# Gate and up weights of an expert in one array: 16384-byte runs in one transfer for the first 48 experts

## What is computed

```python
hb = jax.nn.silu(xb @ we_gate[e]) * (xb @ we_up[e])
return (hb @ we_down[e]).astype(jnp.float32) * wrow[:, None]
```

## Time and profile before

| | |
|---|---|
| three runs | 1462.86, 1464.38 (median), 1465.65 us |
| profiled execution | 1464.3 us, its span 1462.5 us |
| TensorE busy | 1390.4 us (95%) |
| VectorE, ScalarE, POOL busy | 794.4, 372.3, 619.7 us |
| TensorE clock granted, mean | 0.987 |
| DMA | 322.22 MB in 123758 packets; q1 257.80 MB, q0 63.65 MB |
| chain that ended last | DMA 31%, of which the scatters 29%; TensorE 27% |

### The profile page before, as it was taken

How to read it: one execution, slowest core, us unless ns; L and a number is a source line. 1 busy time by engine, 2 the same in 40 slices (tenths; PEclk the granted TensorE clock), 3 DMA queues, 4 the chain that set the end, 5 groups by cost and what they waited for, 6 DMA issues and landing times.

```text
span 1462.5 us, 16744 instructions
## 1 busy us (share of the span) xinstructions
PE 1390.4 (95%) x5222; PEld 717.3 (49%) x5222; DVE 794.4 (54%) x1412; ACT 372.3 (25%) x745; POOL 619.7 (42%) x594
## 2 busy tenths in 40 slices
PE   7999999999997999999899999999999999999993
PEld 3544666666665445554344444444444444444441
DVE  3575999999987337885333433333333333333326
ACT  0314566665565212220001001000100010010116
POOL 0008456665420001344545555554555455656511
PEclk9999999999998999999999999999999999999997
DMA  9506001001122731128699999999999999999948
GB/s 236 80 37 77 17 12 20 16 16 20 44 78 68 282 149 59 59 105 320 259 347 374 369 364 373 372 364 367 373 371 366 368 367 350 360 353 352 345 95 230
DMA packets 123758, 322.22 MB, mean 220 GB/s; under 512 B 47286, under 2 KB 67406, under 8 KB 105266
## 3 DMA queue, kind: packets, MB, share of 16 engines
q1 hardware_dynamic: 99138, 257.80, 48.6%
q0 software_dynamic: 24560, 63.65, 18.1%
HBM read 276.45 MB, written 51.72 MB: 224 GB/s over the span
## 4 chain that ended last, share of the span: by engine, by line
DMA 31%; PE 27%; issue 4%; DVE 3%; SPq 1%; POOLq 0%; ACT 0%; POOL 0%; ACTq 0%; DVEq 0%
DMA sum_d<-moe_y,moe_idx 29%; PE moe_p_gu L1772 11%; PE moe_p_y L1792 5%; PE mix_p_m L1310 4%; PE mix_p_m L1316 4%; PE mix_p_x L1355 1%; PE mix_p_m L1355 1%; DMA expert_d<-mix_where_i 1%; DVE mixers_ring_b L2023 1%; SPq L1129 1%; PE mix_p_log L1335 1%; DVE mixers_ring_b L2018 1%; DMA shared_xg<-x_d,moe_idx 1%; PE moe_p_h L1780 0%; PE mix_p_x L1325 0%
## 5 line engine op out<-in xcount | busy, mean ns | idle before, releaser
L1698 POOL DMA_INDIRECT shared_xg<-x_d,moe_idx x240 | 243.6, 1015 | 107.1 <-issue 55.6
L1935 DVE STREAM_TRANSPOSE moe_xgT<-shared_xg 128x1024 f32<-128x1024 f32 x65 | 132.0, 2031 | 137.4 <-DMA shared_xg<-x_d,moe_idx 130.3
L1709 POOL DMA_INDIRECT sum_d<-moe_y,moe_idx x65 | 105.6, 1624 | 228.3 <-DMA sum_d<-moe_y,moe_idx 194.8
L1952 DVE TENSOR_SCALAR moe_y<-moe_p_y,shared_block_w 128x512 f32<-128x512 f32 x65 | 48.8, 751 | 210.5 <-DMA sum_d<-moe_y,moe_idx 153.3
L1792 PE MATMUL moe_p_y<-mixers_ring_b,moe_hT 128*128 128x512 f32 x352 | 158.2, 592 | 0.0
L1772 PE MATMUL moe_p_gu<-mixers_ring_b,moe_xgT 128*128 128x512 f32 x352 | 154.7, 592 | 0.0
L1772 PE MATMUL moe_p_gu<-all_x_sb,moe_xgT 128*128 128x512 f32 x336 | 147.7, 592 | 0.0
L1264 POOL DMA_INDIRECT slot_d<-all_const,all_dest_i x48 | 48.4, 1009 | 219.7 <-DVE all_dest_i L1523 207.5
L715 PE MATMUL att_p_s<-latents_kT,att_qT 128*128 128x512 f32 x256 | 123.5, 605 | 0.7 <-ACT att_v_last L890 0.7
L1863 ACT ACTIVATE moe_y<-moe_p_y,shared_block_w 128x512 f32<-128x512 f32 x65 | 44.7, 687 | 292.2 <-DMA sum_d<-moe_y,moe_idx 262.9
L1857 ACT ACTIVATE moe_sig<-moe_p_gu 128x256 f32<-128x256 f32 x65 | 24.9, 383 | 349.3 <-PE moe_p_gu L1772 349.3
(11 more groups left out here) (339 smaller groups left out, 2165.6 us busy)
## 6 DMA issues: line engine op xcount, KB each, us to landing
mixers_ring_b<-in_we_down_dram SPq DMA_DIRECT2D x32, 1024.0 KB
mixers_ring_b<-in_we_gate_dram SPq DMA_DIRECT2D x16, 1024.0 KB
mixers_ring_b<-in_we_up_dram SPq DMA_DIRECT2D x16, 1024.0 KB
all_x_sb<-in_we_gate_dram SPq DMA_DIRECT2D x16, 1024.0 KB
all_x_sb<-in_we_up_dram SPq DMA_DIRECT2D x16, 1024.0 KB
mixers_ring_b<-in_we_down_dram SPq DMA_DIRECT2D x24, 512.0 KB
mixers_ring_a<-in_we_gate_dram SPq DMA_DIRECT2D x8, 1024.0 KB
mixers_ring_a<-in_we_up_dram SPq DMA_DIRECT2D x8, 1024.0 KB
```

Source lines behind the costliest of these rows:

```text
L1698: nc.gpsimd.indirect_dma_start(xg[:, u, g, :], None, k.x1_quarters, bass.IndirectOffsetOnAxis(ap=idx[:, c, g:g + 1], axis=0), bounds_check ...
L1709: nc.gpsimd.indirect_dma_start(k.sum_d[:, :], bass.IndirectOffsetOnAxis(ap=idx[:, c, NQ:NQ + 1], axis=0), y[:, u, :], None, compute_op=ALU ...
L1935: nc.vector.transpose(xgT[:, u].rearrange("p k (g i) -> p g k i", g=NQ), xg[:, seat].rearrange("p g (j k) -> p g k j", k=KD)).then_inc(x_t ...
```

## The change

The host hands over one array `we_gu` in place of `we_gate` and `we_up`: for every expert 128 rows (one per partition) of 16384 bytes, 8192 of gate and then 8192 of up. A partition's part of gate is what it was before (8 rows of 256 numbers, contiguous). With `pieces` = 1 one transfer of 2 MB fills the place in runs of 16384 bytes and adds 16 to the semaphore, where two transfers of 1 MB added 32. With `pieces` = 2 there are four transfers of 512 KB in runs of 4096 bytes, as before, in the same order; at the source their runs lie 16384 bytes apart instead of 8192. Down weights, all other work and the number of bytes are the same.

```diff
-        self.we_gate, self.we_up, self.we_down, self.ws_gate = [given[n] for n in ("we_gate", "we_up", "we_down", "ws_gate")]
+        self.we_gu, self.we_down, self.ws_gate = [given[n] for n in ("we_gu", "we_down", "ws_gate")]
...
 def gate_up_landed(rounds):
-    return 32 * min(rounds, WHOLE) + 64 * max(rounds - WHOLE, 0)
+    return 16 * min(rounds, WHOLE) + 64 * max(rounds - WHOLE, 0)
...
 def load_gate_up(eng, k, slot, expert, pieces=1):
 
-    one = bass.ds(expert, 1)
-    for part, w in enumerate((k.we_gate, k.we_up)):
-        rows = w[0].rearrange("e (p q k) f -> e p q (k f)", q=pieces, k=KD // pieces)[one].rearrange("e p q w -> (e p) q w")
-        place = k.moe_gu[slot][:, part, :].rearrange("p (q w) -> p q w", q=pieces)
-        for q in range(pieces):
-            eng.dma_start(place[:, q, :], rows[:, q, :]).then_inc(k.gu_in[slot], 16)
+    runs = 1 if pieces == 1 else 2 * pieces
+    rows = k.we_gu[bass.ds(expert, 1)].rearrange("e p (q w) -> (e p) q w", q=runs)
+    place = k.moe_gu[slot].rearrange("p h w -> p (h w)").rearrange("p (q w) -> p q w", q=runs)
+    for q in range(runs):
+        eng.dma_start(place[:, q, :], rows[:, q, :]).then_inc(k.gu_in[slot], 16)
...
-                pe.wait_ge(k.gu_in[v], n * (64 if c // RING >= WHOLE else 32) + gate_up_landed(c // RING + 1))
+                pe.wait_ge(k.gu_in[v], n * (64 if c // RING >= WHOLE else 16) + gate_up_landed(c // RING + 1))
...
+    pair = [inputs[name].reshape(-1, P, KD * F) for name in ("we_gate", "we_up")]
+    arrays["in_we_gu_dram"] = _np.concatenate(pair, axis=2)
+    aps["we_gu"] = nc.dram_tensor("in_we_gu_dram", arrays["in_we_gu_dram"].shape, f32, kind="ExternalInput").ap()
```

More of the change, by code:

```diff
@@ L2119 @@
     arrays, aps = {}, {}
-    for name in _INS:
+    for name in [name for name in _INS if name not in ("we_gate", "we_up")]:
         a = _np.ascontiguousarray(inputs[name])
```

## The result

The changed kernel took **1480.84 us** (median of 14 runs, 1468.34 to 1490.41) beside 1463.70 us for the kernel before (14 runs, 1460.33 to 1467.09): the ratio is 1.0108, 95% interval 1.0094 to 1.0123. It is slower by 1.1%, 17 us between the medians, and its executions spread over 22 us instead of 7. A ratio leaves out executions that lie more than 1.5% above the fastest of their kernel, here the one of 1490.41 us.

> The changed kernel itself, for a trace nearer to its middle run (the first one took 1490.4 us, the median of 14 is 1480.8).

What follows compares the result with a forecast made beforehand. The scatter loop on POOL's queue and full DMA engines were taken to hold experts at 11.2 us against TensorE's 10.53. Terms -2 - 0.3 - 0.4 + 0.5 = -2 gave about 1462.5 us from 1464.38; range 1452 to 1488.

Steps and rivals of the forecast that it cites:

- the likeliest case: Expert stage before 1190 us: full DMA engines set the floor, about 1462.5 us, range 1455 to 1470; chance 0.45.
- the first rival: Scatter loop at L1709: scatters still pay long turns while engines idle elsewhere, +12 to +45 us, 1476 to 1509; chance 0.27.
- What limits that: Scatter loop: the emptied weights queue lets scatters through, so 41 experts average 11.17 us instead of 11.21, -2 us.
- A swing costs nothing by itself: Expert stage: periods swinging between 10.5 and 12.5 us cost nothing, as POOL is in order and TensorE has the gathers' lead.
- The spacings over 12 us for some five experts: Scatter loop, about 750 to 830 us: spacings of 12 to 13 us, then an uneven pace with mean 11.1 to 11.2.
- The saving of 0.08 us per expert: DMA engines, gate and up loads: 8 packets instead of 16 save 8 x 0.010 us, period 11.21 to 11.13 us.
- The upper bound of 1.4 us: Duration of a 16384-byte packet: at most 1.4 us, from 34 instruction fetches; 0.606 us was taken.
- the formula for the loop with long neighbours alone: Scatter loop: fixed 6.1 us plus 8 turns of 0.327 + 0.606 us gives 13.5 us with 16384-byte neighbours only.
- cut into shorter packets: Rival, gate and up loads: 16384-byte runs are cut into packets of 8192 or less, so nothing changes, 1464 +- 1; chance 0.08.
- the long packet is not slow: Denies the rival that long weight packets are slow as instruction fetches: 1710 us, half the way 1590; chance 0.05.
- No lost pace: Rival, scatter loop: fewer packets and shorter backlog drop it below 10.9 us, 12 to 15 us faster, 1449 to 1452; chance 0.15.
- The start: First loads, list write and slot scatters: -0.4 us for shorter loads, +0.5 (0 to +2) for slower slot scatters.

Runs made afterwards that it cites:

- the kernel with late long runs: 16384-byte gate and up runs for experts 24 to 47 alone, 8192-byte runs in two transfers for 0 to 23: 1477.80 us, 1.0094 of the kernel before.
- the slowest run: The first profiled execution of the changed kernel itself, nothing else altered: 1490.41 us.
- issuing earlier: The changed kernel with SP issuing gate and up of the next expert ahead of down of the last: 1469.64 us, 1.0042 of the kernel before.

## Why the prediction was wrong, point by point

The median of 1480.84 lies within the range (1452 to 1488), but the likeliest case had 1462.5, with slower by over 0.2% at 0.39. What came is the first rival, "the scatter stays behind large packets" (given 0.27, 1476 to 1509): its place is the loop at L1709, its mark a mean spacing of 11.5 to 12.3 (measured 11.50 and 11.73, at the lower end), and its turning point of 11.28 was passed. That the median fell within the range owes nothing to the likeliest case, which had the sign wrong.

- **The step that failed is "What limits that"**, with its two premises. One was that the queue, once it had run empty, would let scatters through and so hold the mean at the work of full engines (11.13 to 11.17 us). In the sum this was the term 41 x (11.17 - 11.21) = -2 us; measured, the 39 spacings from the second scatter on cost +11.7. In part the queue does let scatters through: while a scatter's 128 packets move, about 88 hardware packets start, where it was about 143. But the queue runs empty also while no scatter moves, as at 884 us, and that time is lost. The rival had named this condition; I set it aside because the sum of work argued against it, and a sum of work can't say when the queue is empty. Also missing was any spread between a scatter's packets: its last tenth takes 1.1 us instead of 0.55.
- **"A swing costs nothing by itself" failed too.** TensorE's lead over the gathers is used up by the swing (waits of 5.2 and 5.5 us), TensorE waits and then runs at the lower clock for a while, places come free late and in bursts, and SP's issue stops for 16 us. The prediction had the very row, SP waiting 43 times for TensorE, and read it as a limit on the backlog only.
- **The spacings over 12 us for some five experts** came, later than forecast (from 825 us, not 750 to 830), but they aren't made good later, as the sum had it: in the kernel with late long runs they cost 7.4 us once, and the mean after them is 11.4, where less than 11.2 would be needed to pay them back.
- **The saving of 0.08 us per expert** was about right where no scatter runs (a long packet took 0.618 us there; 0.606 forecast), and is lost beside scatters, where a long packet takes 0.635 us, two short ones 0.640. The term was 1% of the queue's work, and 0.1% came. Why packets are slower there was not settled. (The upper bound of 1.4 us came from a rounded 0.2%; the 34 instruction fetches took 1.10 us each.)
- **What held:** turns packet for packet (69 beside 70); the formula for the loop with long neighbours alone roughly (13.5; seen 14.3); TensorE leaving 10.53 before expert 21 (after the 14th sigmoid, 10th in the slowest run); an uneven pace; nothing in the last 16 experts; no price for the layout. A run is not cut into shorter packets, and the long packet is not slow: these two rivals fell.
- **"No lost pace"**, the rival that went with the page DMA: Bandwidth & Descriptors of the Trainium skill (Anatomy of one DMA, a fixed cost per transfer), fell. One transfer fewer per expert brought no gain in either run length: +0.43% with 8192-byte runs, and with 16384-byte runs 1.0106 in two transfers and 1.0085 to 1.0108 in one.
- **The start:** the slot scatters did get slower, and the gather behind them waited 9.45 us (6.71 in the earlier trace rows):

```profile
692.61 0.90 POOL L1275 DMA_INDIRECT mix_entries<-slot_d,mix_where_i  x1 [9.45 <-DMA slot_d<-all_const,all_dest_i]
```

It is issued 5.2 us later than before, and the sigmoids start 0.8 us later (728.1 against 727.3). That isn't evidence for the +0.5 of the forecast: the first load of weights is issued 2.4 us later too (653.3 us for 650.9), ahead of anything that the change touches, and over the profiled runs of all kernels it lies between 648.2 and 653.7. Counted from that load the sigmoids start 1.6 us earlier in this run and 1.0 us later in the slowest one, so the start has no price that can be told.

The sum as it was measured, for the profiled run of 1475.9 us (+11.6 over 1464.3): start +0.8 (not due to the change, as far as can be told), second to last sigmoid +10.6, the tail about 0. By mechanism, the long turns while a backlog exists make about 7 us (priced in the kernel with late long runs, late last packets included). Idle engines make an estimated 5.4 us, the lower clock at most 5 us, and issuing earlier takes back about half of the whole loss. These overlap and aren't a clean sum. Not settled: why the joined transfer with short runs loses 0.43%, why the last packets of a scatter come late, and how much of the changed kernel's loss is of that kind.

## What to carry to other kernels

Where two queues share DMA engines packet for packet, as here, the run length of the bulk transfer is the length of the turn that every small transfer waits for; if those small transfers form a chain (issue, land, issue), price the chain with both neighbours before lengthening the bulk's runs. That all engines are full, and a work sum at its floor, doesn't protect: ask when the bulk queue can run empty, who refills it and what that engine is waiting for. A wait can cost more than its length when the clock falls with it: read the granted clock behind it. Refill each place as soon as it is free, not in the order in which it is used.

## What the chip showed that was not expected

A weights transfer that covers only the lower or only the upper 64 partitions is far slower than one over all 128 or over every second one: the same bytes and the same 16384-byte runs took 1.2010 [1.1957, 1.2062] of the kernel before in two halves, and 1.0106 [1.0083, 1.0129] split into even and odd partitions; with 8192-byte runs in halves it was 1.1503 [1.1467, 1.1539]. A DMA share near 1.0 doesn't mean full use: it read 1.02 in a stretch in which throughput had fallen by 2%, and 1.01 at 243 GB/s in the kernel with halves, whose long packets took 1.2 us instead of 0.61. The time of a packet that is held up counts as busy.
